# A third buffer of attention probabilities, and turns, values and outputs one unit later

## The reference

```python
# mixer A: causal attention, 4 heads of 64; with 512 tokens and blocks of 256 every past block is selected
s = jnp.where(mask, q @ k.T * 64 ** -0.5, -inf);  out = softmax(s) @ v
# mixer D: 4 heads, two score maps of 32 channels each
s = einsum(q[map], k[map]) * 32 ** -0.5          # causal, per block of 128 queries
p = softmax(where(mask, s, -inf))
out = (p[map 0] - lam * p[map 1]) @ v
```

## Time and profile before

| what | value |
|---|---|
| median of three runs | 1782.45 us |
| profiled execution | 1788.86 us |
| its span | 1787.0 us, 1.86 us less than its time |
| attention loop, layer 0 | about 229.5 to 330.3 us |
| attention loop, layer 1 | about 1105.9 to 1214.0 us |
| PE busy over the span | 88% |
| granted TensorE clock over the span | 0.972 |

### The profile page before, as it was taken

How to read it: one execution, slowest core, us unless ns; L and a number is a source line. 1 busy time by engine, 2 the same in 40 slices (tenths; PEclk the granted TensorE clock), 3 DMA queues, 4 the chain that set the end, 5 groups by cost and what they waited for, 6 DMA issues and landing times.

```text
span 1787.0 us, 22127 instructions
## 1 busy us (share of the span) xinstructions
PE 1574.4 (88%) x9144; PEld 957.7 (54%) x9144; DVE 568.5 (32%) x1294; ACT 291.3 (16%) x706; POOL 158.8 (9%) x175
## 2 busy tenths in 40 slices
PE   7999989999799888777699999999998997987783
PEld 3445766566565454444344557664755564544441
DVE  2165246444121111221422742464432211113115
ACT  3131265220000000000123123451100000000001
POOL 0010000002211111110000100000031110111000
PEclk9999999999999999999899999899999999999997
DMA  9103012548999999999821111026599999999994
GB/s 323 68 35 103 8 48 95 196 198 364 425 423 424 424 424 425 422 424 418 362 96 79 53 59 48 1 95 247 224 376 425 424 424 424 423 424 423 424 418 196
DMA packets 72711, 486.57 MB, mean 272 GB/s; under 512 B 24413, under 2 KB 26397, under 8 KB 37792
## 3 DMA queue, kind: packets, MB, share of 16 engines
q1 hardware_dynamic: 62240, 468.81, 63.9%
q0 software_dynamic: 10368, 16.30, 2.5%
HBM read 472.24 MB, written 30.21 MB: 281 GB/s over the span
## 4 chain that ended last, share of the span: by engine, by line
PE 59%; DMA 29%; DVE 4%; SPq 3%; issue 2%; ACT 2%; POOL 1%; DVEq 0%; POOLq 0%; ACTq 0%
DMA RING<-in_w_up 15%; PE banks L623 13%; PE banks L972 11%; PE banks L612 6%; PE banks L925 5%; PE banks L987 5%; DMA TOK<-in_w_up 4%; DMA RING<-in_w_down 3%; DMA TOK<-in_w_gate 2%; PE banks L950 2%; SPq L491 2%; PE banks L849 2%; PE banks L821 1%; DMA XS<-x_rows,SOLVE 1%; PE banks L965 1%
## 5 line engine op out<-in xcount | busy, mean ns | idle before, releaser
L972 PE MATMUL banks<-RING,XS 128*64 128x256 f32 x2752 | 316.5, 385 | 55.1 <-DMA RING<-in_w_up 35.1
L972 PEld LDWEIGHTS banks<-RING,XS 128*64 128x64 f32 x2752 | 218.3, 138 | 164.8 <-DMA RING<-in_w_up 45.1
L623 PE MATMUL banks<-RING,XNT 128*128 128x512 f32 x512 | 226.0, 599 | 0.2 <-DMA RING<-in_w_in_blocks 0.2
L987 PE MATMUL banks<-RING,XS 128*64 128x512 f32 x768 | 177.4, 603 | 27.3 <-issue 13.5
L1808 DVE SCALAR_TENSOR_TENSOR XS<-banks,TABLE,XS 128x256 f32<-128x256 f32 x58 | 28.1, 484 | 435.8 <-PE banks L972 435.8
L623 PEld LDWEIGHTS banks<-RING,XNT 128*128 128x128 f32 x512 | 97.3, 192 | 118.8 <-issue 117.6
L1286 ACT ACTIVATE XS<-banks,TABLE 128x256 f32<-128x256 f32 x58 | 27.4, 473 | 797.2 <-PE banks L972 797.2
L987 PEld LDWEIGHTS banks<-RING,XS 128*64 128x64 f32 x768 | 60.9, 138 | 111.1 <-issue 111.1
L1850 DVE COPY XS<-banks 128x512 f32<-128x512 f32 x64 | 44.2, 691 | 215.6 <-PE banks L987 190.4
L2026 POOL DMA_INDIRECT y_rows<-XS,SOLVE x64 | 65.2, 1019 | 526.4 <-DVE XS L1850 504.4
L612 PE MATMUL banks<-XNT,RING 128*128 128x512 f32 x256 | 110.2, 592 | 0.0
(11 more groups left out here) (346 smaller groups left out, 1756.8 us busy)
## 6 DMA issues: line engine op xcount, KB each, us to landing
RING<-in_w_down SPq DMA_DIRECT2D x46, 2048.0 KB, 27.3
RING<-in_w_up SPq DMA_DIRECT2D x44, 2048.0 KB, 27.5
RING<-in_w_gate SPq DMA_DIRECT2D x42, 2048.0 KB, 27.0
RING<-in_w_in_blocks SPq DMA_DIRECT2D x12, 2048.0 KB, 10.1
TOK<-in_w_gate SPq DMA_DIRECT2D x12, 2048.0 KB, 32.8
TOK<-in_w_up SPq DMA_DIRECT2D x10, 2048.0 KB, 33.2
XNT<-in_w_down SPq DMA_DIRECT2D x8, 2048.0 KB, 30.9
TOK<-in_w_down SPq DMA_DIRECT2D x6, 2048.0 KB, 24.2
```

Source lines behind the costliest of these rows:

```text
L623: last = mm(bank[:, :], XNT[:, k, i * P:(i + 1) * P], w[:, k, :], start=(k == 0), stop=(k == KD - 1))
L972: last = mm(bank[f * CAP:(f + 1) * CAP, 0:256], rows[:, k, :], w[:, k, f * 256:(f + 1) * 256], start=(k == 0), stop=(k == KD - 1))
L987: last = mm(PS[5][n * CAP:(n + 1) * CAP, :], HT[:, j, f * CAP:(f + 1) * CAP], w[:, k, n * BN:(n + 1) * BN], start=(k == 0), stop=(k == KF ...
```

## The change

`PB` has three buffers, of 1024 columns each: the two old halves and 1024 unused columns of `RING`; the buffer of unit n is n % 3 in place of n % 2. The turn of a unit moves from two to three steps behind its scores, its values from three to four, its output from four to five, and the loop has one step more (37). Maxima, exponentials and weights of the sums stay in their steps, and so does all that stands between steps.

```diff
-        PB = view(XNTb, 2048, 2048, "p (b m t) -> p b m t", b=2, m=2)
+        PB = [view(t, lo, 1024, "p (m t) -> p m t", m=2) for t, lo in ((XNTb, 2048), (XNTb, 3072), (RING, SC0 + 7168))]
...
-            for u in range(len(UNITS) + 4):
+            for u in range(len(UNITS) + 5):
...
-                        if 2 <= u < len(UNITS) + 2:
-                            n = u - 2
+                        if 3 <= u < len(UNITS) + 3:
+                            n = u - 3
...
-                                last = tr(PS[7][:, b * P:(b + 1) * P], PB[:, n % 2, MAPS[n] - 1, b * P:(b + 1) * P], ident)
+                                last = tr(PS[7][:, b * P:(b + 1) * P], PB[n % 3][:, MAPS[n] - 1, b * P:(b + 1) * P], ident)
...
-                        if 3 <= u < len(UNITS) + 3:
-                            n = u - 3
+                        if 4 <= u < len(UNITS) + 4:
+                            n = u - 4
...
-                        if u >= 4:
-                            n = u - 4
+                        if u >= 5:
+                            n = u - 5
...
-                        if 2 <= u < len(UNITS) + 2:
-                            n = u - 2
+                        if 3 <= u < len(UNITS) + 3:
+                            n = u - 3
...
-                                ac(PB[:, u % 2, a, 0:w], PS[SCORE_BANKS[k % 4]][:, 0:w], ACT.Exp, bias=nmx[:, k:k + 1],
+                                ac(PB[u % 3][:, a, 0:w], PS[SCORE_BANKS[k % 4]][:, 0:w], ACT.Exp, bias=nmx[:, k:k + 1],
...
-                                p0, p1 = PB[:, n % 2, 0, 0:w], PB[:, n % 2, 1, 0:w]
+                                p0, p1 = PB[n % 3][:, 0, 0:w], PB[n % 3][:, 1, 0:w]
```

## The result

The changed kernel takes 1789.33 us, the median of 12 runs (1786.19 to 1811.79), the kernel before 1782.49 in 12 runs beside them (1779.72 to 1790.37): 6.8 us more, a ratio of 1.0055 with an interval of [1.0036, 1.0074]. That is slower, and beyond the range. The profiled execution of after took 1789.09 us, near its median.

What follows compares the result with a forecast made beforehand. PE's waits in the two attention loops were taken as the bound; waits gone less new ones gave 1.5 us in layer 0 and 1.6 in layer 1, so 1782.45 less 3.1, some 1779.3 us, range 1771 to 1786.5.

Steps and rivals of the forecast that it cites:

- the term for the clock: Attention loops of both layers: granted clock stays as before, 1.00 and 0.66 in the two stretches; no time counted.
- this rival: Slower by the clock: layer 0's loop up to unit 10's scores loses up to 9.4 us, total 1788.7; chance 0.12.
- runs at the low clock: Layer 1's first loop part: PE's work is longer there, so step 8 gets no new wait; layer gain 1.6 us.
- the sum: PE's waits that go less those that come in both loops: 1.5 us in layer 0, 1.6 in layer 1, together 3.1.
- waits in steps 8 to 12: New PE waits of 0.5 us in the loop, the argument given for a slower result by the clock.
- 0.7 and 0.43: PE's waits after the change: about 0.7 us in step 10; in step 12 0.2 more than the old 0.23.
- the prediction's prices: PE's work per block in the loop: some 0.11 us for a turn, 0.21 us for values.
- Steps 10 to 15: Layer 0's loop: step 10 costs 0.55 us, step 12 costs 0.2, step 15 wins 0.75.
- the 0.3 for step 21: Loop, step 21: the turn's wait of 0.72 us ends; gain taken as 0.3 us because the output comes later.
- the 0.5 that the prediction named as its bound: Prediction counts as wrong if the loop's gain at equal clock is under 0.5 or over 3 us a layer.
- The change doesn't touch this.: ACT's order in the loop: the output stays behind the previous step's exponential, so step 9 gains 0.93 of 1.24 us.

Runs made afterwards that it cites:

- e1: Changed kernel plus one unused 512-column product ahead of unit 4's scores and two ahead of step 5's values, per layer: 1775.05 us.
- e4: Kernel before with three buffers of probabilities and its step order kept: 1781.28 us, ratio 0.9989.
- e8: Changed kernel plus two unused products in step 5's wait of 1.28 us alone: 1775.18 us, ratio 0.9963.
- e5: Kernel before plus three unused products per layer, one ahead of unit 4's scores and two ahead of step 5's values: 1778.04 us.
- e9: Changed kernel plus two unused half-width products in step 6's wait alone: 1780.9 us, ratio 0.999.
- e3: Three buffers; units 0 to 6 turned two steps behind their scores as in the kernel before, units from 7 on three steps: 1778.95 us.
- e6: Kernel before, two buffers, with ACT's output one step earlier, ahead of the exponential: 1774.6 us, ratio 0.9954.
- e2: Changed kernel with ACT's output one step earlier, ahead of the exponential: 1759.12 us, ratio 0.987.

## Why the prediction was wrong

**What failed is the term for the clock,** which the forecast put at nothing: layer 0's loop was to be shorter "at an unchanged clock". Its stretch took 30.80 us at 0.72 instead of 25.40 at 1.00, and without the falls the changed kernel is 14.3 us shorter (e1). The prediction named this rival, its place and nearly its time (1788.7; measured 1789.33), and gave it 0.12 with the sentence that "no row tells which way the change tips it". That the time fits is luck: the rival lets layer 0 go to the 34.80 us of layer 1, while both layers took 30.8 and 30.9.

Two steps were wrong in this. First, layer 0 at 1.00 and layer 1 at 0.66 were taken for a property of the layers; layer 1 "runs at the low clock" entered the sum as a constant. It is a matter of chance in the kernel before: the kernel with three buffers alone (e4), whose order is the same, took 26.78 us for that stretch of layer 1 in its profile, not 34.83. Second, in weighing the rival I counted waits in steps 8 to 12, since they are the ones that the sum moved. I passed over step 5's wait, the longest of the loop, without which the clock doesn't fall there (e1, e8), and over step 6 behind it, where the change takes three blocks of a turn away.

**The sum was too large.** The waits for `probs` went, and those for the output came with 0.71 and 0.45 us where the prediction had 0.7 and 0.43. What is left of the gain is read at one clock, from the starts in e1 and e5. At unit 10's scores the changed kernel still has the turn of unit 7 and the values of unit 6 to do, at the others likewise; by the prediction's prices, 0.11 and 0.21 us a block, that is an estimated 0.86, 0.86, 1.07 and 1.17 us, and nothing at the end. Less this work, layer 0 stands at:

| won up to | forecast, us | measured, us |
|---|---|---|
| unit 10's scores | 0.93 | 0.51 |
| unit 13's scores | 0.18 | -0.24 |
| unit 16's scores | 0.93 | 0.48 |
| unit 22's scores | 1.23 | 0.42 |
| the loop's end | 1.5 | 0.69 |

Steps 10 to 15 went as forecast: 0.75 lost, then 0.72 won. Ahead of unit 10, 0.42 is missing; 0.3 of it is step 6, whose wait is 0.55 us in e1 and 0.23 in e5, and for which the sum had no term. Between units 16 and 22 the 0.3 for step 21 did not come: its wait of 0.72 went, but waits of 0.16 and 0.25 us stand there in e1. Layer 1 ends with 0.20 for 1.6, under the 0.5 that the prediction named as its bound.

So the loops of the two profiled executions show 0.9 us of the forecast 3.1. That the medians differ by 3.0 doesn't bear the sum out: as a whole the profiled execution of e1 (1775.72) is longer than that of e5 (1774.12), and what the rest of the 3.0 is beyond noise stays open.

**The account by medians:** before 1782.5; without its own falls at this place 1778.0 (e5); with the change, 1775.1 (e1); the falls of the changed kernel 14.3 more, 1789.3. That the fall needs step 5's wait is shown by its disappearance in e8. That step 6 makes it more frequent is borne out by the times of e9 and e3 and by the count of loops; the chance of a fall was not measured directly, since only the profiled execution of a kernel has windows. How step 6 does it is not shown: in the changed kernel's layer 0 the clock falls at 242.3, before PE waits in step 6.

The Trainium skill, "TensorE: Matmul & The Clock Gate", section "A second HAM failure mode: psum-queue depth-cycling", says that short idles between groups of matmuls can make the clock swing. This trace agrees: 1.28 us of waiting, then 17 us at 0.50.

**What would have won** was in the prediction too. It says of the output behind the exponential: "The change doesn't touch this." Touching it too brings the changed kernel from 1789.33 to 1759.12 us, 22 under the kernel before (1781.62 in the runs beside it); in the kernel before it is worth 7.0 (e6). In e2 the clock stays at 1.00 up to F3, and PE's loop, from its first scores to the output projection, takes 90.7 and 89.3 us in the two layers against 100.7 in layer 0 before. Of these 10.0 us in layer 0, 6.9 are idle time of PE that went (9.05 to 2.11 by the windows of these stretches); the rest is busy time, with 6.8 us at 0.50 behind F3 in e2 and 10.2 in the kernel before. The Trainium skill, "Perfetto Trace Analysis", section "Matmuls", wants groups rotated through banks; here one bank each was enough, as soon as its copy no longer stood behind other work.

## What to carry to other kernels

Where short products alternate with short waits, add up not only the time of the waits but look at what stands around the longest one: the clock can fall there. Here moving work away from behind that wait went with more falls, and two idle products in the wait were worth more than the reordering. Before adding a buffer, look at which instruction stands ahead of the one that frees the old one; moving that copy up made the buffer pay. One profiled execution of a kernel whose clock swings is a sample: take its stretches at either clock as chances, not as facts of the layer.

## What the runs showed of the hardware that was not expected

Two products of 0.5 us each, in a wait of 1.28 us, saved 14 us. A wait of 1.28 us among short products was followed by 17 us at 0.50 in some loops and by none in others of the same kernel: in the profile of the kernel before it fell behind this wait in layer 1 and not in layer 0. Behind F3's sixteen products, which the trace shows as 1.90 us of busy PE, the clock fell in every loop: no later than 2.5 us after them in 20 of 22, and 6 us after them in two, behind a wait of 1.59 us (e8) and 1.81 us (e6).
